# A two-block transformer kernel with a PEER layer on one core: gate tables read earlier, last picks before dots, gelus later among the picks, third tile first at the end

## The chip, the cores and the metric

One core of a Trainium2 chip runs the whole kernel. The metric is the device time of one execution in microseconds (us); lower is better. A run's time is given as the median of several executions; the profile is one more execution, whose span runs from its first instruction to its last.

## The reference, cut to what matters

The input is one sequence of 512 tokens by 1024. Two blocks are computed one after the other, in float32. The first has two kinds of attention and a dense feed-forward layer, the second an mLSTM, a differential attention and a PEER layer; a final norm ends it. All that the change touches is the PEER layer and the norm behind it:

```python
q = (xb @ w_query).reshape(TOKEN_BLOCK, P_HEADS, 2, P_HALF)
s = jnp.einsum('thpk,hpnk->thpn', q, sub_keys).astype(jnp.float32)
sv, si = lax.top_k(s, P_TOPK)
...
fv, fpos = lax.top_k(cand, P_TOPK)
eidx = jnp.take_along_axis(cidx, fpos, axis=-1)
g = jax.nn.softmax(fv, axis=-1)
u = u_tab[eidx]
act = jax.nn.gelu(jnp.einsum('td,thkd->thk', xb, u).astype(jnp.float32), approximate=False)
return jnp.einsum('thk,thkd->td', (g * act).astype(xb.dtype), v_tab[eidx])
```

Each token picks 128 of 16384 experts (8 heads of 16), each expert a row `u` and a row `v` of 1024 numbers. The 512 tokens are four tiles of 128, numbered 0 to 3. The layer's output is multiplied by `g2` and added to `x`, and the sum goes through an rmsnorm.

## The kernel before, in words

The program is written out by hand for five engines and their queues, with semaphores between them; nothing reorders it. The engines are PE (matmuls), ACT (activations), DVE (vector work), POOL (which issues the indirect gathers) and SP (which only issues transfers).

The PEER layer treats its four token tiles in two ways.

**Picks, tiles 0 and 1.** For each of the 256 picks (2 tiles of 128, `NPICK`), POOL gathers one row of `u` and `v` together for each of 128 tokens, 1 MiB in all, into one of 8 slots (`rows`, line 2351). DVE takes the dot product (`dot`, line 2176), ACT the gelu and its product with the gate (`weights`, lines 1815 and 1816), and DVE adds the weighted `v` row to the tile's sum (`value`, line 2194) three picks later. The slot is then free, and POOL gathers the pick that comes 8 later into it. The first 39 picks (`NEARLY`) belong to an earlier stretch of 20 beats (`NBEAT`), and their values are added by PE with diagonal matrices (`values`, line 1552).

**Dense chunks, tiles 2 and 3.** All 16384 experts are computed for these 256 tokens, in 128 chunks (`NCHUNK`) of 128 experts. Per chunk `c` the work is:

- SP loads a turned `u` block (512 KB, `ubuf`, three buffers, lines 1322 and 1342) and a `v` block (512 KB, `vbuf`, three buffers, line 1325).
- PE makes the dots of chunk `c + 16` (`dense_dots`, line 1591; `AHEAD` is 16).
- ACT takes the gelu of a pair of chunks `m`, that is chunks `2m` and `2m + 1` (`dense_gelu`, line 1844). It waits for the dots of the pair and for the values of the chunk 16 before, whose weights lie in the same buffer (`d_done`).
- DVE multiplies the pair with its gates (`dense_weights`, line 2229). The gates come from 64 tables that PE makes in the last 8 beats (`gate_tables`, line 1614). ACT copies them and stores them to DRAM (line 1837), and SP reads them back as 16 blocks of 1 MiB, each with the gates of 8 chunks (`load_gates`, line 1328).
- PE multiplies the weights with the `v` block into banks 2 to 5, tile 2 into banks 2 and 3 (`td` 0) and tile 3 into banks 4 and 5 (line 1644).

The dots of the first 16 chunks are made ahead of chunk 0: ten in the beats, and chunks 10 to 15 in the last beat, behind its last gate table. The last four early picks, 35 to 38, are added by PE behind those six.

**What ties picks to chunks** is the order on ACT and DVE. `pick_at(c)` is 39 + 1.8 c, the pick that is due at chunk `c`:

```python
while m < NCHUNK // 2 and pick_at(2 * m + 1 - AHEAD) <= n:
    dense_gelu(m)
...
while m < NCHUNK // 2 and n >= max(NEARLY + 2 + m, pick_at(2 * m + 1 - 9)):
    dense_weights(m)
```

The first is ACT's loop over the picks `n` and runs ahead of `weights(n)`; the second is DVE's and runs behind `dot(n)`. PE's dots of chunk `2m + 4` wait for the gelu of pair `m`, whose PSUM bank they overwrite.

At chunks 114 and 118 PE turns `x` of tiles 2 and 3, and ACT copies them behind picks 246 and 253 (line 1887). At the end DVE closes each tile in four steps (`last`, lines 2233 to 2258): times `g2`, plus `x`, sum of squares, and behind ACT's square root the product with the gain. SP stores the tile.

Of the kernel before, what the change touches and what calls it, by code (L numbers as in the profile page):

```python
# [49 lines left out]
NGT = 2  # L50
# [3 lines left out]
AHEAD = 16  # L54
# [35 lines left out]

QBEAT = 9
DOT_PAIRS = {11: 1, 12: 1, 13: 1, 14: 1, 15: 1, 19: 3}
DOT_PAIR0, _seen = {}, 0
# [111 lines left out]
def build(nc, ap, out, gates_in_dram):  # L205
    with ExitStack() as ctx:
# [1082 lines left out]
        s_done, s_ev, w_ok, d_done = sem("dense_dots"), sem("dense_gelu"), sem("dense_weights"), sem("dense_values")  # L1289
        a_pool = sem("first_one_hots_pool")  # L1290
        x_copied = sem("x_copied")
        g2_pe, g2_ev = sem("g2_pe"), sem("g2_ev")
# [18 lines left out]
        def _(sp):  # L1311
            sp.wait_ge(ada_first[3], 16)
            for n in range(NBLK):
                if n >= 2:
                    sp.wait_ge(mm_done, MM_THROUGH[n - 2])
                sp.dma_start(ring[n % 2][:, :], ap["wstream"][n]).then_inc(w_loaded[n % 2], 16)
            for j in range(AHEAD + 3):
                if j == 0:
                    sp.wait_ge(mm_done, MM0["pq"] + 1)
                if j >= 3:  # L1320
                    sp.wait_ge(s_done, j - 2)
                sp.dma_start(ubuf[j % 3], ap["u_turned"][j]).then_inc(u_loaded[j % 3], 16)

            def load_values(j):
# [11 lines left out]
            load_gates(1)  # L1336
            load_values(2)
            for c in range(NCHUNK):
                if c + AHEAD + 3 < NCHUNK:
                    sp.wait_ge(s_done, c + AHEAD + 1)  # L1340
                    j = c + AHEAD + 3
                    sp.dma_start(ubuf[j % 3], ap["u_turned"][j]).then_inc(u_loaded[j % 3], 16)
                if c + 3 < NCHUNK:
                    sp.wait_ge(d_done, c + 1)
                    load_values(c + 3)
                if c % 8 == 0 and c // 8 + 2 < 16:
                    sp.wait_ge(w_ok, 4 * (c // 8 + 1))
                    load_gates(c // 8 + 2)
                if c == 100:
                    sp.wait_ge(fin_ok, 1)  # L1350
                    sp.dma_start(out[0:P, :], acc[0]).then_inc(stored, 16)
# [7 lines left out]
        def _(pe):  # L1359
# [196 lines left out]
            for i, (half, c) in enumerate(QUERIES):  # L1556
# [12 lines left out]
                if i % 2 == 0 and i >= 2:  # L1569
                    key_scores(i // 2 - 1)  # L1570
                if i == 6:
                    pe.wait_ge(tt_ev, 1)
                    for b in range(2):
                        ins = turn(hT, 1, b, 6 + b)
                    ins.then_inc(tt_pe, 1)
                if i == 9:
                    pe.wait_ge(tt_ev, 2)
                    for k in range(KD):
                        ins = pe.matmul(PS[:, 6 + k // 4, tile(k % 4)], modc2[:, 40 + k:41 + k].to_broadcast([P, P]), ident,
                                        start=True, stop=True)  # L1580
                    ins.then_inc(g2_pe, 1)
# [41 lines left out]
            for b in range(QBEAT, NBEAT):  # L1623
# [6 lines left out]
                for g in beat_tables(b):  # L1630
                    gate_tables(g)
            beat_dots(NBEAT - 1)
            values(beat_picks(NBEAT - 1))

            pe.wait_ge(picks_ev, 2)
            pe.wait_ge(g_ev, 64)
            for c in range(NCHUNK):
                if c + AHEAD < NCHUNK:
                    dense_dots(c + AHEAD)
                pe.wait_ge(w_ok, c // 2 + 1)  # L1640
                pe.wait_ge(vt_loaded[c % 3], 16 * (c // 3 + 1))
                for td in range(2):
                    for half in range(2):
                        ins = pe.matmul(bank(2 + 2 * td + half), weights_of(c)[:, tile(td)], vbuf[c % 3][:, half * 512:half * 512 + 512],  # L1644
                                        start=(c == 0), stop=(c == NCHUNK - 1))
                ins.then_inc(d_done, 1)
                if c in (4, 80):
# [7 lines left out]
                if c in (114, 118):  # L1655
# [4 lines left out]
                    for half in range(2):  # L1660
                        ins = turn(xT, 2 + c // 118, half, half)
                    ins.then_inc(x_turned, 1)


        @block.scalar
        def _(act):
# [128 lines left out]
            def copy_query(i):  # L1795
# [4 lines left out]
                if i >= 2 and i % 2 == 0:  # L1800
                    copy_scores(i // 2 - 1)
                if i in (1, 6):
                    t = i // 6
                    act.wait_ge(tt_pe, t + 1)
                    act.activation(h2tok[t].rearrange("p (a n) -> p a n", a=2), PS[:, 6:8, :], ACT.Copy).then_inc(tt_ev, 1)
                if i == 9:
                    act.wait_ge(g2_pe, 1)
# [63 lines left out]
            for n in range(NEARLY, NPICK):  # L1871
                while m < NCHUNK // 2 and pick_at(2 * m + 1 - AHEAD) <= n:
                    dense_gelu(m)
                    m += 1
# [19 lines left out]
        def _(dve):  # L1894
# [336 lines left out]
            def last(t, step):  # L2231
                a = halves(acc[t])
                ss = ssf[t]
                if step == 0:
# [3 lines left out]
                    else:  # L2238
                        dve.wait_ge(d_done, NCHUNK)
                        own(dve.tensor_tensor(a, PS[:, 2 * t - 2:2 * t, :], g2row[:, :, :], ALU.mult))  # L2240
# [40 lines left out]
            for n in range(NEARLY, NPICK):  # L2281
                dot(n)
                while done < min(n + 1 - lag_of(n), NPICK):
                    value(done)
                    done += 1
                while m < NCHUNK // 2 and n >= max(NEARLY + 2 + m, pick_at(2 * m + 1 - 9)):
                    dense_weights(m)
                    m += 1
# [8 lines left out]
            while m < NCHUNK // 2:  # L2297
                dense_weights(m)
                m += 1
            for t, step in ((1, 0), (1, 1), (1, 2), (1, 3), (2, 0), (2, 1), (2, 2), (3, 0), (3, 1), (3, 2), (2, 3), (3, 3)):  # L2300
                last(t, step)
# [178 lines left out]
```

## Time and profile before

| What | us |
|---|---|
| Median of 3 runs (all: 2657.36, 2665.32, 2668.45) | 2665.32 |
| The profiled execution, its own time | 2658.6 |
| Its span, first to last instruction | 2655.9 |
| PE busy | 2491.8 (94%) |
| DVE busy | 1485.2 (56%) |
| ACT busy | 602.3 (23%) |
| POOL busy | 432.5 (16%) |
| Moved by the transfers | 592.31 MB, mean 223 GB/s |

Busy shares are over the whole span. The rows in the section below are of the stretch that the change touches, from about 1700 us to the end; in them a matmul in float32 has two records, and so has a dot on DVE, so that a count of 8 on line 1644 is one chunk and a count of 16 on line 1591 one chunk's dots.

### The profile page before, as it was taken

What the parts mean: (1) busy time and instruction counts of PE and PEld (TensorE: products, weight loads), DVE (VectorE), ACT (ScalarE), POOL (GpSimd) and SP (SyncE); (2) the same over time, 40 slices, a digit from 0 to 9 for tenths busy, and PEclk for the clock granted to TensorE, in tenths of its full rate; (3) what the DMA queues carried; (4) which work ended last, traced back from release to release, by engine and by line L of the source; (5) the groups of instructions that cost most, each with busy time, mean ns of one, the idle gap of its engine ahead of it and who ended that gap; (6) DMA issues with size and microseconds to landing.
All of it is one profiled execution on the core that took longest, in us unless ns stands there. A gap on an engine that the chain in (4) does not pass through costs nothing.

```text
span 2655.9 us, 24709 instructions
## 1 busy us (share of the span) xinstructions
PE 2491.8 (94%) x8808; PEld 1431.0 (54%) x8808; DVE 1485.2 (56%) x3368; ACT 602.3 (23%) x1482; POOL 432.5 (16%) x351
## 2 busy tenths in 40 slices
PE   6999999999999999999998887799999999999997
PEld 3454555444444444444467665666665666656563
DVE  5444454220105424223657799847686877777777
ACT  2022364110000002222422245501111112111111
POOL 0000000000000000000000155523333333333331
PEclk9999999999999999999999998999999999999999
DMA  9531011112127521111032376889999999999996
GB/s 378 230 119 60 36 48 48 64 67 91 63 108 302 196 90 64 63 64 64 16 143 104 112 280 238 300 356 415 412 417 406 417 416 417 414 417 415 416 396 259
DMA packets 120740, 592.31 MB, mean 223 GB/s; under 512 B 10000, under 2 KB 42768, under 8 KB 76592
## 3 DMA queue, kind: packets, MB, share of 16 engines
q0 software_dynamic: 40656, 321.93, 29.9%
q1 hardware_dynamic: 46224, 247.48, 24.1%
q10 hardware_dynamic: 33744, 21.40, 2.7%
q8 instruction: 67, 1.10, 0.2%
q14 instruction: 49, 0.40, 0.0%
HBM read 571.90 MB, written 18.87 MB: 222 GB/s over the span
## 4 chain that ended last, share of the span: by engine, by line
PE 79%; DMA 10%; DVE 8%; ACT 1%; issue 1%; POOL 0%; DVEq 0%; ACTq 0%; POOLq 0%
PE PS L622 25%; PE PS L1591 13%; PE PS L1644 13%; PE PS L652 8%; DMA arena<-in_u_turned 5%; PE PS L1164 4%; DMA arena<-in_peer_uv 4%; PE PS L1210 3%; PE PS L807 2%; PE PS L1552 1%; PE PS L827 1%; PE PS L816 1%; DMA arena<-in_ada 1%; DVE arena L2219 1%; PE PS L1185 1%; PE PS L1614 1%
## 5 line engine op out<-in xcount | busy, mean ns | idle before, releaser
L1591 PE MATMUL PS<-hT,arena 128*128 128x256 f32 x2048 | 479.6, 389 | 32.6 <-DMA arena<-in_u_turned 32.5
L1591 PEld LDWEIGHTS PS<-hT,arena 128*128 128x128 f32 x2048 | 397.7, 195 | 146.8 <-DMA arena<-in_u_turned 55.5
L2351 POOL DMA_INDIRECT arena<-in_peer_uv,arena x163 | 219.3, 1346 | 1000.2 <-DVE arena L2147 470.2
L622 PE MATMUL PS<-arena,ring 128*128 128x512 f32 x832 | 359.2, 593 | 2.1 <-issue 0.8
L622 PE MATMUL PS<-hT,ring 128*128 128x256 f32 (+1 forms) x928 | 302.7, 486 | 2.9 <-ACT hT L442 2.9
L622 PEld LDWEIGHTS PS<-arena,ring 128*128 128x128 f32 x832 | 157.0, 190 | 203.2 <-issue 201.9
L622 PEld LDWEIGHTS PS<-hT,ring 128*128 128x128 f32 x928 | 179.6, 195 | 122.4 <-issue 105.0
L2194 DVE SCALAR_TENSOR_TENSOR arena<-arena 128x1024 f32<-128x1024 f32 x134 | 171.8, 1282 | 129.3 <-ACT arena L1816 129.1
L1644 PE MATMUL PS<-arena,hT 128*128 128x512 f32 x512 | 231.5, 595 | 6.3 <-DMA arena<-in_peer_uv 4.6
L1644 PE MATMUL PS<-arena,ring 128*128 128x512 f32 x512 | 230.1, 593 | 1.4 <-DMA arena<-in_peer_uv 0.8
L2176 DVE CUSTOM_DVE_ANT_0 arena<-arena 128x1024 f32<-128x1024 f32 x163 | 198.3, 1221 | 44.9 <-DMA arena<-in_peer_uv,arena 44.3
L652 PE MATMUL PS<-hT,ring 128*128 128x512 f32 x512 | 221.5, 595 | 1.7 <-ACT hT L442 1.7
L652 PEld LDWEIGHTS PS<-hT,ring 128*128 128x128 f32 x512 | 97.8, 191 | 124.9 <-issue 123.6
L2351 POOL DMA_INDIRECT ring<-in_peer_uv,arena x93 | 118.3, 1273 | 246.3 <-DVE arena L2194 195.2
L2318 POOL DMA_DIRECT2D arena<-in_ada x20 | 10.5, 528 | 896.2 <-ACTq L406 665.0
L1644 PEld LDWEIGHTS PS<-arena,hT 128*128 128x128 f32 x512 | 95.3, 190 | 110.5 <-issue 108.5
L1644 PEld LDWEIGHTS PS<-arena,ring 128*128 128x128 f32 x512 | 96.4, 190 | 102.7 <-issue 99.6
L2194 DVE SCALAR_TENSOR_TENSOR arena<-ring,arena 128x1024 f32<-128x1024 f32 x81 | 103.9, 1282 | 67.7 <-ACT arena L1816 67.6
L1995 DVE TENSOR_SCALAR arena<-PS 128x512 f32<-128x512 f32 x32 | 22.1, 692 | 195.4 <-PE PS L652 195.4
L1981 DVE SCALAR_TENSOR_TENSOR xT<-PS,modc,xT 128x512 f32<-128x512 f32 x24 | 18.0, 751 | 179.5 <-PE PS L622 179.5
L2176 DVE CUSTOM_DVE_ANT_0 ring<-ring,arena 128x1024 f32<-128x1024 f32 x93 | 113.2, 1220 | 8.1 <-DMA ring<-in_peer_uv,arena 5.6
L1164 PE MATMUL PS<-hT,ring 128*128 128x512 f32 x256 | 115.4, 593 | 0.0
(349 smaller groups left out, 2765.5 us busy)
## 6 DMA issues: line engine op xcount, KB each, us to landing
ring<-in_wstream SPq DMA_DIRECT2D x45, 2048.0 KB, 7.9
arena<-in_u_turned SPq DMA_DIRECT2D x128, 512.0 KB
arena<-in_peer_uv SPq DMA_DIRECT2D x128, 512.0 KB, 14.7
arena<-in_ada POOLq DMA_DIRECT2D x24, 2048.0 KB, 9.7
gate_tables<-arena ACTq DMA_DIRECT2D x16, 1024.0 KB, 5.3
arena<-gate_tables SPq DMA_DIRECT2D x16, 1024.0 KB, 15.7
arena<-in_peer_uv,arena POOLq DMA_INDIRECT x163
xT<-in_xT POOLq DMA_DIRECT2D x1, 2048.0 KB, 18.9
```

Of the source, the lines that this page charges most:

```text
L622: ins = pe.matmul(o, l, r, start=(a == 0), stop=(a == len(lhs) - 1))
L652: ins = pe.matmul(bank(j % 2, n), w[:, k, m * P:(m + 1) * P], act_in(k), start=(k == 0), stop=(k == kc - 1))
L807: ins = pe.matmul(o, l, r, start=True, stop=True)
L816: ins = pe.transpose(o, l, ident[0:n, 0:n])
L827: ins = pe.matmul(o, l, r, start=start, stop=stop)
L1164: ins = pe.matmul(bank(7), w[:, k, tile(j % 4)], hT[:, k, :], start=(k == 0), stop=(k == KD - 1))
L1210: ins = pe.matmul(bank(5 + j % 2), lhs, rhs, start=(k == 0), stop=(k == KD - 1))
L1591: ins = pe.matmul(dense_bank(j), ubuf[j % 3][:, tile(k)], hT[:, k, 256:512], start=(k == 0), stop=(k == KD - 1))
L1644: ins = pe.matmul(bank(2 + 2 * td + half), weights_of(c)[:, tile(td)], vbuf[c % 3][:, half * 512:half * 512 + 512], start=(c == 0), stop=( ...
L2176: dve.tensor_tensor_reduce(u, u, h2tok[t], 1.0, 0.0, ALU.mult, ALU.add, dots[:, e:e + 1]).then_inc(dot_ok, 1)
L2194: ins = dve.scalar_tensor_tensor(out=a, in0=v, scalar=wexp[:, t, e:e + 1], in1=a, op0=ALU.mult, op1=ALU.add)
L2351: pool.indirect_dma_start(rows[j], None, ap["peer_uv"], bass.IndirectOffsetOnAxis(ap=eidx[:, t, e:e + 1], axis=0)).then_inc(landed[j], 16)
```

## The change

Five edits, all of order; no instruction is added but for one more semaphore.

1. **Turns of tokens.** In the queries' loop PE turns the tokens of tile 1 behind query 3 instead of 6, and `g2` behind query 5 instead of 9. ACT's copies of them move alike.
2. **SP's queue.** The `u` blocks 0 to 12 are issued as before. Then come `v` block 0, gate block 0, `v` block 1, gate block 1 and `v` block 2, and only then the `u` blocks 13 to 18, which wait for the dots of chunks 10 to 15.
3. **Last early picks.** PE adds the values of picks 35 to 38 before the dots of chunks 10 to 15.
4. **Gelus and their products.** ACT's place for `dense_gelu(m)` is `pick_at(2m + 1 - 12)`, was `- 16`; DVE's for `dense_weights(m)` is `pick_at(2m + 1 - 7)`, was `- 9`.
5. **The end.** In the last three chunks (`LAST`) PE does tile 2's half alone; tile 3's three halves follow. DVE waits for tile 2's matmuls with a semaphore of their own, and does all of tile 2's steps before tile 3's.

```diff
-            for j in range(AHEAD + 3):
-                if j == 0:
-                    sp.wait_ge(mm_done, MM0["pq"] + 1)
+            def load_first_rows(j):
                 if j >= 3:
                     sp.wait_ge(s_done, j - 2)
                 sp.dma_start(ubuf[j % 3], ap["u_turned"][j]).then_inc(u_loaded[j % 3], 16)
+
+            sp.wait_ge(mm_done, MM0["pq"] + 1)
+            for j in range(2 * DOT_PAIR0[NBEAT - 1] + 3):
+                load_first_rows(j)
...
             load_gates(1)
             load_values(2)
+            for j in range(2 * DOT_PAIR0[NBEAT - 1] + 3, AHEAD + 3):
+                load_first_rows(j)
...
-                if i == 6:
+                if i == 3:
                     pe.wait_ge(tt_ev, 1)
...
-                if i == 9:
+                if i == 5:
                     pe.wait_ge(tt_ev, 2)
...
+            values(beat_picks(NBEAT - 1))
             beat_dots(NBEAT - 1)
-            values(beat_picks(NBEAT - 1))
...
-                for td in range(2):
-                    for half in range(2):
...
-                ins.then_inc(d_done, 1)
+                ins = second_rows(c, 0)
+                if c == NCHUNK - 1:
+                    ins.then_inc(d_first, 1)
+                if c < NCHUNK - LAST:
+                    second_rows(c, 1).then_inc(d_done, 1)
...
+            for c in range(NCHUNK - LAST, NCHUNK):
+                second_rows(c, 1).then_inc(d_done, 1)
...
-                while m < NCHUNK // 2 and pick_at(2 * m + 1 - AHEAD) <= n:
+                while m < NCHUNK // 2 and pick_at(2 * m + 1 - 12) <= n:
                     dense_gelu(m)
...
-                while m < NCHUNK // 2 and n >= max(NEARLY + 2 + m, pick_at(2 * m + 1 - 9)):
+                while m < NCHUNK // 2 and n >= max(NEARLY + 2 + m, pick_at(2 * m + 1 - 7)):
...
-            for t, step in ((1, 0), (1, 1), (1, 2), (1, 3), (2, 0), (2, 1), (2, 2), (3, 0), (3, 1), (3, 2), (2, 3), (3, 3)):
+            for t, step in ((1, 0), (1, 1), (1, 2), (1, 3), (2, 0), (2, 1), (2, 2), (2, 3), (3, 0), (3, 1), (3, 2), (3, 3)):
```

How the instructions stand on SP around the last gate table. In the names, `in_u_turned` is a `u` block, `in_peer_uv` a `v` block and `gate_tables` a gate block; `dense_dots` is the semaphore of the chunks' dots. Before:

```order
L1322 DMA arena<-in_u_turned 128x1024 [waits dense_dots] x16
L1325 DMA arena<-in_peer_uv 128x1024 [waits gate_tables]
L1328 DMA arena<-gate_tables 128x2048 [waits gate_table_stored1,gate_table_stored0]
L1325 DMA arena<-in_peer_uv 128x1024
L1328 DMA arena<-gate_tables 128x2048
L1325 DMA arena<-in_peer_uv 128x1024
L1342 DMA arena<-in_u_turned 128x1024 [waits dense_dots]
```

And now:

```order
L1322 DMA arena<-in_u_turned 128x1024 [waits dense_dots] x10
L1329 DMA arena<-in_peer_uv 128x1024 [waits gate_tables]
L1332 DMA arena<-gate_tables 128x2048 [waits gate_table_stored1,gate_table_stored0]
L1329 DMA arena<-in_peer_uv 128x1024
L1332 DMA arena<-gate_tables 128x2048
L1329 DMA arena<-in_peer_uv 128x1024
L1322 DMA arena<-in_u_turned 128x1024 [waits dense_dots] x6
L1348 DMA arena<-in_u_turned 128x1024 [waits dense_dots]
```

Six loads of `u` blocks have moved behind the five reads of values and gates.

PE behind the last gate table (line 1614). Line 1591 is the dots of a chunk, line 1552 the value of an early pick. Before, with the six chunks' dots cut to the first and the last:

```order
L1614 MATMUL PS<-arena 128x128 x3
L1591 MATMUL PS<-hT,arena 128x256 [waits dense_gelu,u_loaded1]
...
L1591 MATMUL PS<-hT,arena 128x256 [waits u_loaded0]
L1591 MATMUL PS<-hT,arena 128x256 x7
L1552 MATMUL PS<-ring,arena 128x512 [waits diagonals]
```

And now, where these lines are 1620, 1597 and 1558:

```order
L1620 MATMUL PS<-arena 128x128 x3
L1558 MATMUL PS<-ring,arena 128x512 [waits diagonals]
...
L1558 MATMUL PS<-arena 128x512 [waits diagonals]
L1558 MATMUL PS<-arena 128x512
L1597 MATMUL PS<-hT,arena 128x256 [waits dense_gelu,u_loaded1]
```

The four picks' values stand ahead of the six chunks' dots.

The last two gelus on ACT (pairs 62 and 63), up to the copy of tile 2's `x` (line 1887). Line 1844 is the gelu of a pair, lines 1815 and 1816 are one pick, and the pick that also waits for `gates` is pick 240. Before:

```order
L1844 ACTIVATE ring<-PS 128x512 [waits dense_values,dense_dots]
L1815 ACTIVATE arena<-arena 128x1 [waits dots]
L1816 ACTIVATE arena<-arena 128x1 [waits act_own]
...
L1844 ACTIVATE ring<-PS 128x512 [waits dense_values,dense_dots]
...
L1815 ACTIVATE arena<-arena 128x1 [waits dots,gates]
...
L1887 ACTIVATE arena<-PS 128x1024 [waits x_turned]
```

And now, where these lines are 1858, 1829, 1830 and 1901:

```order
L1829 ACTIVATE arena<-arena 128x1 [waits dots,gates]
...
L1858 ACTIVATE ring<-PS 128x512 [waits dense_values,dense_dots]
...
L1858 ACTIVATE ring<-PS 128x512 [waits dense_values,dense_dots]
L1829 ACTIVATE arena<-arena 128x1 [waits dots]
L1830 ACTIVATE arena<-arena 128x1 [waits act_own]
L1901 ACTIVATE arena<-PS 128x1024 [waits x_turned]
```

Both gelus stood ahead of pick 240 and stand behind it now; between the last gelu and the copy there were nine picks and is one.

## Rows read from the trace of the kernel before

**Rows 1.** The page's 40 slices of the span: PE and transfers, in tenths
```profile
PE   6999999999999999999998887799999999999997
DMA  9531011112127521111032376889999999999996
```
**Rows 2.** Stretches: length, busy of each engine (count), clock, DMA share, GB/s
```profile
1720.00:2579.20 859.20, 823.75 (x2807) 537.17 (x2806) 616.90 (x1111) 149.88 (x507) 281.18 (x203) 0.98 1.01 409
1718.00:1745.00 27.00, 27.00 (x112) 20.94 (x111) 0.46 (x2) 3.06 (x6) 2.89 (x3) 1.00 0.65 213
1748.00:1758.00 10.00, 10.00 (x34) 6.27 (x33) 4.48 (x7) 0.00 (x0) 0.94 (x1) 1.00 1.02 425
```
**Rows 3.** Stretches again, the long middle and the two of the end
```profile
1760.00:2570.00 810.00, 774.55 (x2624) 502.43 (x2623) 607.52 (x1098) 146.98 (x500) 273.60 (x196) 0.98 1.02 415
...
2579.20:2621.40 42.20, 37.31 (x98) 16.29 (x96) 32.60 (x41) 9.94 (x35) 12.74 (x10) 1.00 0.98 392
2621.40:2642.30 20.90, 20.82 (x48) 8.98 (x48) 13.17 (x17) 2.48 (x6) 0.00 (x0) 1.00 0.41 134
```
**Rows 4.** Up to 2579.2, line 2176 alone: DVE busy (dots, two records each)
```profile
0.00:2579.20 2579.20, 295.54 (x484) 0.98 0.57 222
```
**Rows 5.** Up to 2579.2, line 1644 alone: PE and PEld busy (chunks, eight records each)
```profile
0.00:2579.20 2579.20, 404.52 (x897) 168.30 (x898) 0.98 0.57 222
```
**Rows 6.** Up to 1717.6 and up to 2579.2, line 2351 alone: POOL busy (gathers issued)
```profile
0.00:1717.60 1717.60, 43.74 (x43) 0.98 0.35 128
...
0.00:2579.20 2579.20, 324.92 (x246) 0.98 0.57 222
```
**Rows 7.** Who waited for whom, 1745 us to the end: total, times, longest
```profile
ACT hT L1844 <- PE PS L1644: 365.9, 28, 19.8
POOL arena L2351 <- DVE arena L2194: 352.0, 128, 11.7
ACT ring L1844 <- PE PS L1644: 278.3, 24, 16.9
...
DVE arena L2194 <- ACT arena L1816: 196.7, 51, 12.6
...
PE PS L1591 <- DMA arena<-in_u_turned: 32.5, 9, 5.0
```
**Rows 8.** Order of time, 1713 to 1752 us: start, us, engine, line, idle before
```profile
1717.63 20.89 PE L1591 MATMUL PS<-hT,arena 128*128 128x256 f32 x96
...
1718.92 0.37 ACTq L1837 DMA_DIRECT2D gate_tables<-arena  x1
1721.28 17.59 SPq L1322 DMA_DIRECT2D arena<-in_u_turned  x6
...
1738.35 3.60 PE L1552 MATMUL PS<-ring,arena 128*128 128x512 f32 x8
...
1740.50 0.99 POOL L2351 DMA_INDIRECT ring<-in_peer_uv,arena  x1 [23.93 <-PE PS L1552]
...
1747.54 0.69 DVE L2229 TENSOR_TENSOR hT<-hT,arena 128x512 f32<-128x512 f32 x1 [29.08 <-DMA arena<-gate_tables]
```
**Rows 9.** The chain that ended last, in order of time: start, us, what
```profile
2107.58 3.47 PE PS L1591 x16
2111.06 22.48 DMA arena<-in_u_turned
...
2195.46 3.43 PE PS L1644 x8
2198.90 3.45 PE PS L1591 x16
...
2609.16 0.87 PE PS L1530 x8
```
**Rows 10.** Order of time, from 2621 us: start, us, engine, line, idle before
```profile
2621.38 20.84 PE L1644 MATMUL PS<-arena,ring 128*128 128x512 f32 x48 [0.17 <-DMA arena<-in_peer_uv]
...
2629.59 1.22 DVE L2237 TENSOR_TENSOR arena<-arena,sq 128x1024 f32<-128x1024 f32 x1
...
2633.99 1.28 DVE L2257 SCALAR_TENSOR_TENSOR arena<-arena,smalls 128x1024 f32<-128x1024 f32 x1
...
2642.26 1.22 DVE L2240 TENSOR_TENSOR arena<-PS,sq 128x1024 f32<-128x1024 f32 x1 [6.98 <-PE PS L1644]
...
2651.54 1.28 DVE L2257 SCALAR_TENSOR_TENSOR arena<-arena,smalls 128x1024 f32<-128x1024 f32 x1
```

**Rows 11.** ACT in order of time, 1380 to 1400 us, beside the queries
```profile
1384.40 1.02 ACT L1805 ACTIVATE arena<-PS 128x1024 f32<-128x1024 f32 x1 [0.28 <-PE PS L1530]
...
1391.31 0.38 ACT L1799 ACTIVATE arena<-PS 128x256 f32<-128x256 f32 x1 [3.07 <-PE PS L622]
```

More of the change, by code:

```diff
@@ L91 @@
 QBEAT = 9
+LAST = 3
 DOT_PAIRS = {11: 1, 12: 1, 13: 1, 14: 1, 15: 1, 19: 3}
@@ L1290, in build @@
         a_pool = sem("first_one_hots_pool")
+        d_first = sem("dense_values_first_tile")
         x_copied = sem("x_copied")
@@ L1631, in _, with second_rows @@
                     gate_tables(g)
+            values(beat_picks(NBEAT - 1))
             beat_dots(NBEAT - 1)
-            values(beat_picks(NBEAT - 1))
             pe.wait_ge(picks_ev, 2)
             pe.wait_ge(g_ev, 64)
+            def second_rows(c, td):
+                for half in range(2):
+                    ins = pe.matmul(bank(2 + 2 * td + half), weights_of(c)[:, tile(td)], vbuf[c % 3][:, half * 512:half * 512 + 512],
+                                    start=(c == 0), stop=(c == NCHUNK - 1))
+                return ins
             for c in range(NCHUNK):
@@ L1641, in _ @@
                 pe.wait_ge(vt_loaded[c % 3], 16 * (c // 3 + 1))
-                for td in range(2):
-                    for half in range(2):
-                        ins = pe.matmul(bank(2 + 2 * td + half), weights_of(c)[:, tile(td)], vbuf[c % 3][:, half * 512:half * 512 + 512],
-                                        start=(c == 0), stop=(c == NCHUNK - 1))
-                ins.then_inc(d_done, 1)
+                ins = second_rows(c, 0)
[3 more added lines that the diff above has]
+                    second_rows(c, 1).then_inc(d_done, 1)
                 if c in (4, 80):
@@ L1801, in copy_query @@
                     copy_scores(i // 2 - 1)
-                if i in (1, 6):
-                    t = i // 6
+                if i in (1, 3):
+                    t = i // 3
                     act.wait_ge(tt_pe, t + 1)
                     act.activation(h2tok[t].rearrange("p (a n) -> p a n", a=2), PS[:, 6:8, :], ACT.Copy).then_inc(tt_ev, 1)
-                if i == 9:
+                if i == 5:
                     act.wait_ge(g2_pe, 1)
@@ L2238, in last @@
                     else:
-                        dve.wait_ge(d_done, NCHUNK)
+                        if t == NGT:
+                            dve.wait_ge(d_first, 1)
+                        else:
+                            dve.wait_ge(d_done, NCHUNK)
                         own(dve.tensor_tensor(a, PS[:, 2 * t - 2:2 * t, :], g2row[:, :, :], ALU.mult))
```

## The prediction

> **What bounds the kernel now.** I read the slices first. From about 1740 us PE and the transfers both stand at nine tenths or more [rows 1], so either could be the bound. The stretches decide it. Between 1720 and 2579.2 us, the end of chunk 111 (897 records of line 1644 are 112 chunks [rows 5]), 859.2 us at 409 GB/s moved 351 MB [rows 2]. That can be counted out of the program: 115 `v` blocks and 115 `u` blocks of 0.524 MB, 16 gate blocks of 1.049 MB, and gathers 43 to 245, which are 203 of 1.049 MB [rows 6], make 350 MB, and one table's store makes 351. PE's own work is shorter. A chunk is 3.45 us of dots and 3.43 us of values [rows 9], 6.88 us, and PE idled 35 of 810 us [rows 3]. What a chunk must move, 1.05 MB of blocks, 0.13 of gates and 1.8 gathers of 1.05, is 3.07 MB, or 7.4 us at the 415 GB/s of [rows 3]. So up to chunk 111 the kernel is bound by bytes, not by a wait, and a reordering gains there only where the transfers were idle.
>
> Two places are left. From 1718 to 1745 the transfers were busy 0.65 of 27 us [rows 2], so 9.5 us were idle. At the end it turns round. Behind chunk 111 PE has 16 chunks without dots left, 16 x 3.43 = 54.9 us and two turns of 0.87 [rows 9]. The first ten and both turns took 42.2 us [rows 3] where PE's work is 36.0, because the last ten gathers were still coming in; the last six ran as one block of 20.84 us [rows 10] with the transfers at 0.41 [rows 3]. Bytes moved before chunk 111 ends cost their full time; bytes left for later cost little.
>
> The waits look like something else. ACT waited 644 us for PE in front of gelus [rows 7], and so DVE for ACT and POOL for DVE. That says only that the picks always stood as far ahead of the chunks as ACT's order lets them.
>
> **Edit 1, the early turns: 0.** The moved copies are 1.02 us on an ACT that idles about 3 us between two queries' copies [rows 11], and PE's work is the same. First used they are only at query 11.
>
> **Edits 2 and 3, the front: -2.5 us.** Before, the gathers of picks 43 to 46 waited for the four values that PE put behind 20.89 us of dots: POOL idled 23.93 us until 1740.5. SP's reads of gates stood behind `u` block 18, and DVE idled 29.08 us for them [rows 8]. Now PE does the four values from 1717.6 to 1724.5, so four gathers leave 20 us earlier, and SP asks for the gates once the last table, on its way since 1718.9 [rows 8], has landed. But the queue is not free: `u` blocks 13 to 15 now stand behind 3.7 MB. From 1718 until block 15 has landed, 5.2 MB of blocks and gates and 4.2 MB of gathers go through, 22.7 us at 415 GB/s; with the store ahead of them this ends near 1747. Dots 13 start then at about 1744.5 and dots 15 end at 1755, against 1738.5 before. On ACT the gelus of pairs 5 to 7 stand ahead of pick 39's weight, so no value is added and no gather beyond pick 46 leaves before 1756 or so. From 1747 to 1758 only `u` blocks 16 to 18 move, 3.8 us of bytes: some 7 us idle in place of 9.5. Ends: -9.5 if everything is filled, +3 if block 13 lands 5 us later. I take the count. PE starts chunk 0 ten microseconds later, which its 35 us of idle time covers; without them it would cost those 10.
>
> **Edit 4, the later gelus: +17.7 and -6.2.** Gelu `m` waits for chunk `2m - 15`. Before, it stood at the pick due at chunk `2m - 15`, now at the one due at `2m - 11`. The picks may so run four chunks, 7.2 picks, further ahead, and as they stood at this limit all the way [rows 7] I expect them to take it. At the end of chunk 111 gelu 63 held pick 238: 242 dots were done [rows 4] and 246 gathers issued [rows 6]. Now it holds pick 246, value 245 has freed its slot, and 254 are issued. The last four of them leave at the end of chunk 109, two chunks of 6.88 us earlier, time for 5.7 MB of which 2.1 are blocks, so one may still be under way. Seven more gathers ahead of the end of chunk 111 are 7.3 MB or 17.7 us (ends: 0 if the picks don't move ahead, 20.2 for eight). Behind it, three gathers are left and not ten, and the 42.2 us shrink to PE's 36.0: -6.2 (ends -6.2 and 0). PE's dots need a gelu from chunk `2m - 12` on, so ACT must now be over one chunk ahead; at the new limit it has two to spare. DVE's products come two chunks later in the picks, covered by the same lead.
>
> **Edit 5, the end: -4.4 us.** From PE's last matmul both tiles took DVE from 2642.26 to 2652.82 [rows 10], 10.6 us. One tile alone, by tile 1's steps from 2629.59 to 2635.27 [rows 10], takes 5.7. Tile 2's matmuls now end 3 x 3.43 / 2 = 5.1 us before PE's end, so its 5.7 us run 0.5 past it and tile 3's 5.7 follow: 6.2 in place of 10.6. Ends: -5.1 and 0 (DVE still busy with picks, which it was until 2629.6 [rows 10]).
>
> **Sum:** -2.5 + 17.7 - 6.2 - 4.4 = +4.6 us. The profiled execution took 2658.6, so it would take 2663.2. It lies 6.7 below the median of the three runs, which spread over 11; the mean of the four is 2662.4, and from it I give **2667**.
>
> **Rivals.**
>
> *The picks stay where they were* (the lead is not taken): -2.5 - 4.4 = -6.9, or -13.9 with the front wholly filled; from 2662.4 that is 2655.5 and 2648.5. It would need gathers that get less than their 61% of the bytes. Against it: while PE waited for one 0.5 MB block it took 22.48 us [rows 9], so the gathers crowd the blocks out. Chance 0.18.
>
> *The transfers go faster when they come less in bursts.* 425 GB/s stands in one stretch against 415 in the long one [rows 2, 3]; 2.4% of 810 us is -19.4, with the sum -14.8: 2647.6. Against it: the share is 1.01 to 1.02 all the way, with nothing to fill. Chance 0.09. The Trainium skill, DMA: Bandwidth & Descriptors, Specifications, gives 435 GB/s as the ceiling of the fabric. By that the stretch is 5% from full, and an estimate from that figure is 37 us of gain in place of the 19.4; no row here shows 435 held.
>
> *Not what it says* (the lead and the stalls cancel, or only the end's edit works): 0 to -4.4, 2658 to 2662. Chance 0.13.
>
> *Slower: the lead is paid in full and nothing comes back.* Eight gathers, +20.2, crowd out `u` blocks 126 and 127 and the `v` blocks of chunks 112 to 114, PE enters the last 16 chunks with empty buffers and stalls as before (0), and the front, where pick 39 waits for `u` block 15, gives 0: with the end's edit +15.8, so 2678. It decides from the point where lead and front together cost 17.7 more than the stalls give back. For it: before, `v` blocks came in late down to chunk 121. Chance 0.15.
>
> **How the numbers follow.** A measurement of this kernel can tell about 0.5%, 13.3 us, from no change. Forecast 0.45, rivals 0.18, 0.09, 0.13 and 0.15. Faster by over 13.3 us: most of the second rival and part of the first, 0.16. Slower by over that: two thirds of the last rival and the forecast's upper ends, 0.13. The rest, 0.71, is within. The range 2650 to 2681 leaves out most of the second rival and the last one's extreme.
>
> **What would show it.** In the profile after: the wait of 29 us for the gate tables on DVE and POOL's of 24 gone, but a wait of PE for a `u` block at dots 13 and transfers nearly idle around 1750; gelus waiting for PE as before; at the end of chunk 111 about 250 dots and 254 gathers, at about 2594; then all 16 chunks in 57 us; 6.2 us of DVE behind PE's last matmul. The forecast is wrong if the count of gathers there is still about 246, or if the middle moves more than 420 GB/s.

## The result, and the profile after

The changed kernel takes **2679.86 us** (median of 6 runs, 2673.52 to 2681.16), the kernel before 2663.82 (6 runs, 2657.36 to 2668.45). The ratio is 1.0056, 95% interval 1.0046 to 1.0066: slower by 12.3 to 17.6 us. The forecast was 2667, 4.6 us more than its base of 2662.4. The time lies inside the range, but where the slower rival had put it (2678), and with parts that neither had summed.

| What | us |
|---|---|
| The profiled execution, its own time | 2679.83 |
| Its span | 2678.0 |
| PE busy | 2500.6 (93%) |
| DVE busy | 1485.2 (55%) |
| ACT busy | 603.7 (23%) |
| POOL busy | 420.7 (16%) |
| Moved by the transfers | 592.33 MB, mean 221 GB/s |

The profiled execution of before (2658.6) was a short one for its kernel, 5 us under the median of 2663.8. From the last gate table to the end of chunk 111 it took 861.4 us; the two experiments that are before's up to there (the turns alone and the end alone) took 868.4 and 870.4, but their profiled executions lay 2 and 7 us over their own medians. A difference between two profiles in this stretch is thus known to some 9 us only. The rates of the first 80 us and the counts agree far better.

Stretches of after. The first is the 80 us behind the last gate table, the next two are inside it, then come the picks' first long stretch, the middle, all of it up to the end of chunk 111, and the 42.2 us behind that, as in [rows 2, 3].

```profile
1721.30:1801.30 80.00, 68.86 (x255) 49.38 (x255) 36.31 (x62) 10.96 (x37) 16.54 (x15) 0.91 0.85 324
...
1745.00:1755.00 10.00, 5.36 (x13) 4.30 (x14) 0.19 (x2) 0.00 (x0) 0.00 (x0) 0.50 0.63 259
...
1765.00:1780.00 15.00, 15.00 (x55) 10.19 (x54) 14.77 (x21) 2.92 (x13) 6.14 (x5) 1.00 0.87 326
...
1840.00:2100.00 260.00, 239.54 (x794) 152.85 (x793) 197.72 (x359) 47.25 (x159) 82.90 (x65) 0.97 1.02 416
...
1760.00:2570.00 810.00, 772.25 (x2609) 499.58 (x2608) 615.23 (x1107) 150.44 (x503) 266.65 (x199) 0.98 1.01 411
...
1721.00:2610.30 889.30, 835.29 (x2820) 542.84 (x2819) 638.30 (x1138) 157.30 (x525) 282.82 (x211) 0.97 1.00 405
...
2610.30:2652.50 42.20, 42.20 (x111) 19.52 (x111) 25.67 (x31) 8.33 (x25) 3.35 (x2) 1.00 0.69 226
```

Before, the first and the fourth of these:

```profile
1717.80:1797.80 80.00, 75.05 (x280) 53.13 (x279) 30.29 (x47) 9.29 (x31) 16.23 (x14) 0.98 0.89 348
...
1840.00:2100.00 260.00, 249.86 (x847) 163.54 (x846) 196.32 (x358) 45.58 (x155) 90.32 (x65) 0.97 1.01 413
```

The last column is what to read. The first 80 us moved 324 GB/s in place of 348, which is 1.9 MB or 4.6 us at 415. Between 1840 and 2100 the transfers are as full as before, and PE idles 20 of 260 us in place of 10. It does 33 chunks (794 records, 24 to a chunk with its dots) in place of 35, while POOL and DVE have as many instructions as before: here the picks take part of their lead. Behind chunk 111 PE never idled in 42.2 us, where it idled 4.9 before [rows 3].

What was done at the end of chunk 111, at 2610.3: dots on DVE (two records each), chunks on PE (eight each), gathers on POOL, as in [rows 4 to 6].

```profile
0.00:2610.30 2610.30, 305.20 (x500) 0.98 0.57 222
...
0.00:2610.30 2610.30, 404.97 (x897) 168.14 (x898) 0.98 0.57 222
...
0.00:2610.30 2610.30, 325.56 (x254) 0.98 0.57 222
```

So 250 dots and 254 gathers, the two counts that the prediction gave. The waits from 1745 us on, as in [rows 7]:

```profile
POOL arena L2368 <- DVE arena L2208: 356.4, 128, 12.8
ACT ring L1858 <- PE PS L1645: 330.5, 28, 20.1
ACT hT L1858 <- PE PS L1645: 253.2, 23, 17.7
...
PE PS L1597 <- DMA arena<-in_u_turned: 50.2, 11, 11.1
POOL arena L2368 <- DVE arena L2202: 36.3, 1, 36.3
```

ACT still waits 584 us for PE before gelus, 644 before; a POOL wait of 36.3 us is new, and so is one of 11.1 us of PE. Both are in the front. Order of time there, as in [rows 8]:

```profile
1721.11 3.60 PE L1558 MATMUL PS<-ring,arena 128*128 128x512 f32 x8
...
1722.40 0.37 ACTq L1851 DMA_DIRECT2D gate_tables<-arena  x1
1723.27 0.99 POOL L2368 DMA_INDIRECT ring<-in_peer_uv,arena  x1 [4.84 <-PE PS L1558]
...
1738.20 0.33 SPq L1332 DMA_DIRECT2D arena<-gate_tables  x1
...
1743.35 0.69 DVE L2243 TENSOR_TENSOR hT<-hT,arena 128x512 f32<-128x512 f32 x1 [21.22 <-DMA arena<-gate_tables]
...
1749.64 16.84 PE L1597 MATMUL PS<-hT,arena 128*128 128x256 f32 x64 [11.14 <-DMA arena<-in_u_turned]
...
1764.11 1.28 DVE L2202 SCALAR_TENSOR_TENSOR arena<-arena,PS 128x1024 f32<-128x1024 f32 x1 [18.93 <-ACT arena L1830]
...
1765.67 0.94 POOL L2368 DMA_INDIRECT arena<-in_peer_uv,arena  x1 [36.31 <-DVE arena L2202]
```

The chain through it:

```profile
1722.40 15.72 DMA gate_tables<-arena
...
1740.34 9.26 DMA arena<-in_u_turned
```

The last table's store took 15.72 us to land. SP stood behind it, then put two `v` and two gate blocks ahead of `u` block 13, and PE waited for that block until 1749.64. Pick 39's value, and with it the next gather, came at 1764 to 1765.7. Before, they came at 1749.3 and 1750.8:

```profile
1749.30 1.28 DVE L2188 SCALAR_TENSOR_TENSOR arena<-arena,PS 128x1024 f32<-128x1024 f32 x1
...
1750.84 0.94 POOL L2351 DMA_INDIRECT arena<-in_peer_uv,arena  x1 [4.25 <-DVE arena L2188]
```

The end, as in [rows 9, 10]: PE's last blocks, the first step of tile 2, and the last step of tile 3.

```profile
2639.33 20.76 PE L1645 MATMUL PS<-arena,ring 128*128 128x512 f32 x48
2661.70 7.10 PE L1645 MATMUL PS<-arena,ring 128*128 128x512 f32 x16 [1.60 <-DMA arena<-in_peer_uv]
```

```profile
2663.69 1.23 DVE L2257 TENSOR_TENSOR arena<-PS,sq 128x1024 f32<-128x1024 f32 x1 [16.84 <-PE PS L1645]
...
2673.70 1.29 DVE L2274 SCALAR_TENSOR_TENSOR arena<-arena,smalls 128x1024 f32<-128x1024 f32 x1
```

DVE runs 6.2 us past PE's last matmul (2668.8 to 2675.0), as forecast. But PE now waits 1.60 us for the last `v` block.

### The profile page after: what moved, and what is told of

Its sections match the earlier page's. It is cut to its first block, busy times and chain, and to the rows that moved or that the text cites. A ratio compares the mean times of both kernels' runs of the same rounds, so it can differ in the third digit from the quotient of the medians.

```text
span 2678.0 us, 24709 instructions
## 1 busy us (share of the span) xinstructions
PE 2500.6 (93%) x8808; PEld 1434.8 (54%) x8808; DVE 1485.2 (55%) x3368; ACT 603.7 (23%) x1482; POOL 420.7 (16%) x351
## 2 busy tenths in 40 slices
DMA packets 120741, 592.33 MB, mean 221 GB/s; under 512 B 10000, under 2 KB 42768, under 8 KB 76592
## 4 chain that ended last, share of the span: by engine, by line
PE 74%; DMA 15%; DVE 8%; ACT 1%; issue 1%; POOL 0%; SPq 0%; DVEq 0%; ACTq 0%; POOLq 0%
PE PS L623 25%; PE PS L1645 11%; PE PS L1597 11%; PE PS L653 8%; DMA arena<-in_u_turned 8%; DMA arena<-in_peer_uv 5%; PE PS L1165 4%; PE PS L1211 3%; PE PS L808 2%; PE PS L828 1%; PE PS L817 1%; DMA arena<-in_ada 1%; DVE arena L2233 1%; PE PS L1558 1%; PE PS L1186 1%; PE PS L1620 1%
```

## The experiments

Theory: the parts have the prices of the prediction, and the front is worth little either way. Rival: the front costs, because what moves ahead holds up what now stands behind. Kernels are timed against before on the same chip. From here on "front" is GB/s in the 80 us behind the last gate table; kernels with the old front have 344 to 348, and I take 347. A front of X costs 80 x (347 - X) / 415 us. The rule is coarse: with the window 4 us later, one kernel's front reads 280 in place of 270, which is 2 us.

### Each part alone

**Edit 4 alone.**

```diff
-                while m < NCHUNK // 2 and pick_at(2 * m + 1 - AHEAD) <= n:
+                while m < NCHUNK // 2 and pick_at(2 * m + 1 - 12) <= n:
...
-                while m < NCHUNK // 2 and n >= max(NEARLY + 2 + m, pick_at(2 * m + 1 - 9)):
+                while m < NCHUNK // 2 and n >= max(NEARLY + 2 + m, pick_at(2 * m + 1 - 7)):
```

> The kernel before with the later gelus and products alone (edit 4). Theory of bytes: the picks run four chunks further ahead, about 254 gathers are issued when chunk 111 ends in place of 246, that end comes 17 to 20 us later, the 16 last chunks take 57 us in place of 63, and the time is 11 to 14 us longer (ratio 1.004 to 1.005). Rival, that the front alone made the change slower: no difference, within 3 us.

Measured: 2675.69 against 2664.45, ratio 1.0045 (1.0032 to 1.0058), +12.0 us. Its stretch behind chunk 111, then dots and gathers up to there:

```profile
2605.40:2662.10 56.70, 56.66 (x144) 25.60 (x143) 25.67 (x31) 8.33 (x25) 3.35 (x2) 1.00 0.58 199
...
0.00:2605.40 2605.40, 305.30 (x500) 0.98 0.57 223
...
0.00:2605.40 2605.40, 325.60 (x254) 0.98 0.57 223
```

The 16 chunks took 56.7 us with PE busy throughout, and the counts are those predicted. The theory of this part holds, with its size.

**Edits 2 and 3 together**, then each alone. Edit 3 is the first hunk, edit 2 the rest.

```diff
-            beat_dots(NBEAT - 1)
             values(beat_picks(NBEAT - 1))
+            beat_dots(NBEAT - 1)
...
-            for j in range(AHEAD + 3):
...
+            for j in range(2 * DOT_PAIR0[NBEAT - 1] + 3):
+                load_first_rows(j)
...
             load_values(2)
+            for j in range(2 * DOT_PAIR0[NBEAT - 1] + 3, AHEAD + 3):
+                load_first_rows(j)
```

> The kernel before with the gate reads ahead of u blocks 13 to 18 and the last picks' values ahead of the dots (edits 2 and 3). Theory: in the profile after, the last gate table's store landed 15.7 us after its issue, beside the gathers that now start 20 us earlier, and the gate reads, u block 13 and pick 39's weight stand behind it; the front idles as much as it gains, so 0 to +4 us, with the transfers idle around 1750 as in the profile after. Rival, that filling the gap pays as meant: -6 to -10 us.

> The kernel before with the last picks' values ahead of the dots alone (edit 3). Theory: four gathers leave 20 us earlier into transfers that were half idle, and u blocks 13 to 18 keep their place, so PE's dots 10 to 15 end at about 1745 without a wait for a block; pick 39's weight moves from 1739 to 1745 only. The 9.5 us of idle time shrink by about 6: -4 to -8 us. Rival, that the gathers hold up the store of the last gate table here too and that this delays chunk 0: 0 or more.

> The kernel before with the gate reads ahead of u blocks 13 to 18 alone (edit 2). Theory, as the front runs so far have it (lone edit 3 idled the transfers 7.8 us more in the first 80 us, edits 2 and 3 together 11.5 us more): without the early gathers the last gate table's store lands in about 6 us, the gate reads start near 1725, u block 13 comes behind them near 1735, so dots 15 end near 1745, and the gathers of picks 43 to 46, behind those dots as before, leave near 1748 and so still cover the wait of gelu 8 for chunk 1. Idle about as before, 0 to +5 us. Rival, that the edit that hurts is this one, not edit 3: +8 us or more.

| Kernel | ratio (95%) | us | front, GB/s | its cost by the rule above |
|---|---|---|---|---|
| edits 2, 3 | 1.0048 (1.0036 to 1.0061) | +12.8 | 281 | 12.7 |
| edit 3 | 1.0035 (1.0023 to 1.0048) | +9.3 | 302 | 8.7 |
| edit 2 | 1.0051 (1.0036 to 1.0067) | +13.6 | 287 | 11.6 |

The theory fails for all three. For edits 2 and 3 together its rival, a gain, failed too; for each edit alone the rival, a cost, had the sign right. Each part alone costs, and both together cost about what either does: the three intervals overlap. Edit 3 alone, 80 us and 15 us of stretches, then order of time (the last row is pick 39's value):

```profile
1720.90:1800.90 80.00, 67.58 (x238) 46.78 (x238) 28.00 (x39) 7.52 (x25) 15.61 (x13) 0.91 0.79 302
...
1765.00:1780.00 15.00, 15.00 (x55) 10.20 (x54) 7.94 (x11) 2.14 (x9) 3.42 (x3) 1.00 0.41 143
```

```profile
1750.64 0.36 SPq L1328 DMA_DIRECT2D arena<-gate_tables  x1
...
1758.70 2.07 PE L1644 MATMUL PS<-arena,hT 128*128 128x512 f32 x2 [5.55 <-DVE hT L2229]
...
1759.70 1.28 DVE L2188 SCALAR_TENSOR_TENSOR arena<-arena,PS 128x1024 f32<-128x1024 f32 x1
```

The dots of chunks 10 to 15 come 7 us later, and so do the `u` loads that wait for them and the gate reads behind those on SP, at 1750.6. Chunk 0 begins at 1758.7. SP did not stand behind the store here, so it is the order on PE and not the store that costs. Then there is a second hole that the prediction did not have: with the old place of gelus, gelu 8 stands early among the picks and waits for chunk 1, and from 1765 to 1780 the transfers are busy 0.41. POOL idled 11.9 us there, until 1774.1. Edit 2 alone, order of time:

```profile
1723.99 0.37 ACTq L1841 DMA_DIRECT2D gate_tables<-arena  x1
1731.05 0.33 SPq L1330 DMA_DIRECT2D arena<-gate_tables  x1
...
1742.49 12.65 PE L1595 MATMUL PS<-hT,arena 128*128 128x256 f32 x48 [9.28 <-DMA arena<-in_u_turned]
...
1757.13 0.99 POOL L2355 DMA_INDIRECT ring<-in_peer_uv,arena  x1 [37.13 <-PE PS L1556]
```

Here the gates are read at 1731, only 7 us behind their store, and yet PE waits 9.28 us for `u` block 13, since SP issued it behind two `v` blocks and two gate blocks. That wait stands in the path of everything: dots, early values, gathers (POOL idle 37 us), chunk 0 at 1765.3.

**Edit 5 alone, and edit 1 alone.**

```diff
+            for c in range(NCHUNK - LAST, NCHUNK):
+                second_rows(c, 1).then_inc(d_done, 1)
```

> The kernel before with the end's edit alone (edit 5): tile 2's matmuls first in the last three chunks. Theory: DVE behind PE's last matmul shrinks from 10.6 to 6.2 us, nothing else moves: -4.4 us (ratio 0.9983). Rival, that DVE is still busy with picks or the split of the last chunks costs PE: 0.

Measured: 2661.39, ratio 0.9991 (0.9981 to 1.0001), -2.4 us where -4.4 was expected. The interval, -5.1 to +0.3 us, shuts out neither 0 nor -4.4; what tells is the profile. From PE's last matmul to the span's end it is 9.3 us, was 13.7. Part of it was given back in front of it:

```profile
2650.13 7.10 PE L1641 MATMUL PS<-arena,ring 128*128 128x512 f32 x16 [1.69 <-DMA arena<-in_peer_uv]
```

The last three chunks' tile 2 halves take 1.7 us each, so PE reaches the last `v` block 3.4 us after it freed that block's buffer; the load takes longer. A wait at the last `v` block is there in the changed kernel (1.60) and with all but edit 4 (1.44) too, and not in before [rows 10]. -4.4 + 1.7 is -2.7.

```diff
-                if i == 6:
+                if i == 3:
```

> The kernel before with the earlier turns alone (edit 1). Theory: the copies lie in ACT's idle time, nothing waits: 0, within 2 us. Rival, that it is behind the 3 to 4 us by which the last gate table ended later in the profile after: +3 to +4 us (but that also stood in the profiles of the runs without edit 1).

Measured: 2664.46, ratio 1.0005 (0.9995 to 1.0016): nothing, as expected.

**All but edit 4.** The changed kernel with both lines of edit 4 put back.

```diff
-                while m < NCHUNK // 2 and pick_at(2 * m + 1 - 12) <= n:
+                while m < NCHUNK // 2 and pick_at(2 * m + 1 - AHEAD) <= n:
```

> The change without edit 4 (edits 1, 2, 3 and 5). Theory: the front's +12 of the run with edits 2 and 3, less the end's 2 to 4: +8 to +10 us, with 246 gathers when chunk 111 ends and about 20 us idle in the first 80. Compared with the whole change (+15) edit 4 then costs only 5 to 7 us here, since it pays back part of the front's second hole, where alone it cost 11. Rival, that the edits add up: +12 - 3 + 0 = +9 as well, but then the whole change would have had to be +20.

Measured: 2673.53 against 2662.62, ratio 1.0040 (1.0025 to 1.0055), +10.7 us. By the ratios edit 4 thus costs some 4 us on top of the others (1.0056 against 1.0040, give or take 5), and 12 alone. The front is 270, a cost of 14.8, where the changed kernel has 324 and 4.4. The reason is the second hole: in this kernel the transfers were busy 0.38 from 1765 to 1780, in the changed one 0.87. Its last table came 5 us earlier, but from 1760 to 1775 the share is 0.43 too. Later gelus let the picks through.

```profile
1765.00:1780.00 15.00, 15.00 (x56) 10.19 (x55) 6.95 (x9) 2.14 (x9) 2.92 (x2) 1.00 0.38 138
```

### Can the parts be put to better use

**Late gelus only at first.** Edits 2 and 3, and edit 4's places up to pair 12, then back by one chunk a pair to the places of before, for gelus and products.

```diff
-                while m < NCHUNK // 2 and pick_at(2 * m + 1 - AHEAD) <= n:
+                while m < NCHUNK // 2 and pick_at(2 * m + 1 - 12 - min(4, max(0, m - 12))) <= n:
```

> Edits 2 and 3 as in the front run, with edit 4's later places for the first pairs only; from pair 12 on they go back to the places of before. Theory: the second hole of the front, where pick weights wait for gelu 8 and this for chunk 1 while all gathers have landed, closes as it did in the change, and the end of chunk 111 has 246 gathers as before: the idle time of the first 80 us falls from 21 to about 13 us and the time from +12 to +3 to +5 us. Rival, that the front costs its 12 us in another way (PE's late chunk 0): +12 stays.

Measured: 2671.21, ratio 1.0032 (1.0019 to 1.0044), +8.5 us, twice what was expected. The front is 321, a cost of 5.0: the later gelus close the second hole here as well. Some of the rest may lie between 1840 and 2100:

```profile
1840.00:2100.00 260.00, 249.85 (x846) 162.42 (x845) 186.11 (x345) 45.63 (x152) 80.31 (x59) 0.98 1.01 408
```

408 against before's 413 is 1.3 MB or 3.1 us. Kernels with nothing changed here go from 410 to 415, so this is at the edge of what can be told. From 1880 to 1900, where the picks fall back, it is 345.

**Gelus earlier than before**, the opposite of edit 4, with edit 5: the offset grows from 16 chunks to 20.

```diff
+                while m < NCHUNK // 2 and pick_at(2 * m + 1 - AHEAD - min(4, (m - AHEAD // 2) // 4)) <= n:
...
+                while m < NCHUNK // 2 and n >= max(NEARLY + 2 + m, pick_at(2 * m + 1 - 13)):
```

> The opposite of edit 4, with edit 5: gelus at the pick due at chunk 2m - 19 (reached stepwise over the first 16 pairs), products at the one due at 2m - 12. Theory of bytes: the picks stay four chunks further back, about 239 gathers are issued when chunk 111 ends in place of 246, that end comes 17 us earlier, the last 16 chunks stall more (gathers still come) and take 68 to 73 us in place of 63, and with the end's edit the time is 8 to 14 us shorter than before (ratio 0.995 to 0.997). Rival, that edit 4's cost was the picks' order as such or the missing overlap of ACT and PE: slower, as any move from the tuned place.

Measured: 2659.60, ratio 0.9991 (0.9980 to 1.0003), where -8 to -14 us were expected. Chunk 111 ended at 2567.4, 849.0 us behind the last table where kernels with the old lead took 861.4 to 870.4: a gain was there. Behind it the span went on for 90.3 us, where those took 74.5 to 76.7, and most of that is one wait:

```profile
2608.45 1.97 PE L1532 MATMUL PS<-cst,xT 128*128 128x128 f32 x8 [12.02 <-ACT arena L1897]
```

At the second turn of `x`, PE waited 12 us for ACT's first copy, which stands behind a pick that now comes late.

**Two chunks earlier, with that copy moved.**

```diff
+                while m < NCHUNK // 2 and pick_at(2 * m + 1 - AHEAD - min(2, (m - AHEAD // 2) // 4)) <= n:
...
-                if c in (114, 118):
+                if c in (114, 124):
...
-                if n in (pick_at(114) + 2, pick_at(118) + 2):
-                    td = int(n > pick_at(114) + 2)
+                if n in (240, 255):
+                    td = int(n > 240)
```

DVE's products stand at `pick_at(2m + 1 - 11)` here.

> As the run with earlier gelus, but two chunks back in place of four, with edit 5, and with tile 3's turn of x moved from chunk 118 to 124 and ACT's copies of x behind picks 240 and 255. In the run before, PE waited 12 us at that turn for ACT's copy behind pick 246. Theory: 243 gathers when chunk 111 ends, 7 to 8 us earlier, no wait at the turn, last 16 chunks 63 to 66 us: -7 to -11 us. Rival, that the last picks' DVE work now sets the end: -3 to -4 only, the end's edit alone.

Measured: 2660.44 against 2662.62, ratio 0.9984 (0.9972 to 0.9996): by the ratio 4.3 us faster than before, by the medians 2.2. It is the one kernel here whose whole interval (-7.5 to -1.1 us) lies below before, one of twelve tried, and edit 5, which it holds, measured -2.4 alone. The wait at the turn is gone. The gain is less than expected since the limit moved to DVE, as the rival had it:

```profile
2636.58 4.06 DVE L2204 SCALAR_TENSOR_TENSOR arena<-arena 128x1024 f32<-128x1024 f32 x3
...
2656.28 1.28 DVE L2270 SCALAR_TENSOR_TENSOR arena<-arena,smalls 128x1024 f32<-128x1024 f32 x1
```

The last values of picks end at 2640.6, and three tiles of closing steps follow without a gap, 17 us of them; PE had ended at 2643.3. Chunk 111 ended 856.0 us behind the last table, and 83.2 us followed it: what the picks gave back before chunk 111, they took behind it.

**A front that does not stall, and the same with the lead brought back.** Edit 3, but the gelus of pairs 5 to 7 stand ahead of picks 42, 44 and 46, and the first four products come five picks later; later gelus at first as above. The second kernel falls back by six chunks in place of four (products by four in place of two), with edit 5 and the moved copies.

```diff
-            m = AHEAD // 2
+            m = DOT_PAIR0[NBEAT - 1]
...
+                while m < NCHUNK // 2 and (42 + 2 * (m - 5) if m < 8 else pick_at(2 * m + 1 - 12 - min(4, max(0, m - 12)))) <= n:
...
+                while m < NCHUNK // 2 and n >= max(NEARLY + (7 if m < 4 else 2) + m, pick_at(2 * m + 1 - 7 - min(2, max(0, m - 12)))):
```

> The front mended: edit 3, with the weights of picks 39 to 41 ahead of gelu 5 and two picks ahead of each of gelus 6 and 7, the products of pairs 0 to 3 five picks later, and later gelus up to pair 12 as in the run that goes back to the places of before. SP's order is that of before. Theory: values 39 to 43 free slots while PE makes dots 10 to 15, so gathers 47 to 51 fill the hole that a lone edit 3 left, and the idle time of the first 80 us falls from 17.5 to 3 to 6 us, below the 9.7 of before: -3 to -7 us. Rival, that chunk 0, later still behind slower gate reads and u blocks, sets the time: +5 or more.

> Both of the last two: the mended front, gelus two chunks back from pair 18 on, the end's edit and the later turn. Theory: the gains add, -10 to -16 us, faster than both kernels. Rival: DVE behind the last pick sets the end, no better than the better of the two.

Measured: 2663.78 against 2662.62, ratio 1.0000 (0.9986 to 1.0014), and 2669.18, ratio 1.0021 (1.0010 to 1.0032). Both missed, the second with its sign. The first one's stretches, then the second's:

```profile
1721.10:1801.10 80.00, 69.32 (x254) 47.64 (x253) 48.37 (x88) 12.04 (x41) 20.39 (x18) 0.94 0.98 387
...
1840.00:2100.00 260.00, 254.64 (x882) 167.90 (x881) 183.91 (x342) 45.38 (x152) 81.32 (x59) 0.99 0.99 401
```

```profile
1840.00:2100.00 260.00, 252.21 (x869) 165.17 (x868) 169.27 (x321) 44.12 (x146) 71.88 (x53) 0.99 0.96 383
```

The front was mended: 387 GB/s for 347 is 7.7 us gained. But 401 for 413 over 260 us is 3.1 MB, 7.5 us, lost. In 20 us steps the loss is one hole, right where the picks fall back by four chunks within four pairs: 250 GB/s from 1860 to 1880, 385 from 1880 to 1900, and 413 to 418 after it. PE was busy all 40 us, so it could not do more chunks in that time, and with the picks held back the transfers were left without work. In the second kernel the hole is longer (248, 341, 321 and 345 GB/s from 1860 to 1940). With earlier gelus than before, where four chunks were handed back over 16 pairs, there was no such hole: 412 GB/s with PE busy 259.8 of the same 260 us. The fronts of these kernels differ too, so that the pace alone makes the hole is likely and not shown.

For the second kernel the rule of bytes does not close. 30 GB/s over 260 us would be 18.8 us lost, against some 8 for the front and 7.6 for three picks fewer (243 gathers) at chunk 111. But chunk 111 ended 861.9 us behind the last table, as in before (861.4) and 6 to 9 us sooner than in the two other kernels with the old lead. Behind it 84.1 us followed in place of 74.5 to 76.7. There the rival came true: DVE's last value ends at 2646.8, 17 us of closing steps follow without a gap, and PE ends at 2649.3.

## Where the prediction was right and where it was wrong, point by point

**What bounds the kernel: right.** Up to chunk 111 it is bytes: 405 GB/s over 889.3 us are 360 MB, against 351 before, and 8 dots more, whose rows have landed, are 8.4 MB. In the four kernels with edits 2, 3 or both and the old gelus, the bytes of the first 80 us, turned into time at 415 GB/s, give the measured difference within 2 us (for the one with edit 5 too, 14.8 less 2.7 against 10.7). Chunk 111 ended at 2610.3 and not at about 2594: 3.5 us of it are a later last table, which over all fourteen profiles ends between 1716.0 and 1722.9 whatever the edits, the rest the front and the short base.

**Edit 1, 0: right** (1.0005, with its interval).

**Edits 2 and 3, -2.5: wrong, and the step that failed.** The prediction put it so: "with the store ahead of them this ends near 1747. Dots 13 start then at about 1744.5 and dots 15 end at 1755", and "some 7 us idle in place of 9.5". The trace has dots 13 at 1749.64 and pick 39's value, which waits for dots 15 and ACT, at 1764.11. By its front of 324 the changed kernel lost 4.4 us here in place of gaining 2.5. Two things were missing.

- The store was not ahead of the gathers. It shared with them, took 15.72 us, and SP stood behind it. The prediction's own bound allowed block 13 to be 5 us late, and it was; but that bound ended at +3, when the pick's value and so the next gather came 8 us and more after the 1756 that it had. From 1753 to 1757 nothing moved at all.
- The idle time was counted only up to about chunk 0 (1758). With gelus in their old place there is a second hole behind it, at gelu 8. It is why the front costs 12.8 us without edit 4; with it, 4.4 by the front's rate. The signs had it in part: PE's wait at dots 13 and the idle transfers around 1750 came. But DVE's wait for the gates, which was to be gone, fell only from 29.08 to 21.22, and in place of POOL's 23.93 stands one of 36.31.

**Edit 4, +11.5: right.** Alone +12.0 (8.5 to 15.5), with 250 dots and 254 gathers, and 56.7 us for 16 chunks where 57 were given. In the changed kernel they took 58.5, the difference being edit 5's wait. That the picks take any lead they are given held in both directions: 254 gathers at chunk 111 with later gelus, 246 before, 239 with earlier ones. The stretch from the last table to chunk 111 was 884.9 us with edit 4 alone, 861.4 to 870.4 before, and 849.0 with earlier gelus. That is +15 to +24 and -12 to -21 us, which fits 2.5 us for each 1 MiB pick and does not measure it better.

**Edit 5, -4.4: half right.** DVE's part came out as worked out; PE's wait for the last `v` block, which it had at nothing, took 1.6 of it. Measured -2.4.

**The sum.** Put together from what the runs show, front 4.4, gelus 12.0 and end -2.9 are +13.5; measured were +12.3 to +17.6. The forecast's +4.6 was short by 7 us of front, 1.5 of end and 0.5 of gelus; that leaves 1.5 us, within the interval.

**The rivals.** "The picks stay where they were" fell by the counts. "The transfers go faster" fell: the middle went at 411 GB/s, before at 415 [rows 3]. The Trainium skill, DMA: Bandwidth & Descriptors, Specifications, gives 435 GB/s as the fabric's ceiling; in no kernel of this study does a stretch of 200 us go above 417. None of the orders tried here won any of the 4% that are left to it. The slower rival gave the right time from the wrong parts: the stalls behind chunk 111 did come back in full, and the front, which it had at 0, cost in their place. The range held because it reached to that rival; that the time fell into it was luck.

## What to carry to other kernels

Where a queue is bound by bytes, judge a reordering by the bytes moved in the stretch it touches, over a window long enough to hold the second hole, and not by the wait that it removes. When a load is moved ahead of another on a queue that blocks on waits, ask for the last event that the new front load needs (here a store's landing beside gathers), since everything behind it, and the engine that feeds on that, inherits it. Where one stream has a lead over another and the transfers are full, hand it back slowly, no faster than the other stream's engine can use the bytes: here four chunks within four pairs left a hole, four over 16 pairs did not. And look at where the lead comes due: each pick left for later is DVE's work at the end.

## What was not expected of the hardware

- **A store beside gathers.** The same 1 MiB store of the last table took 15.72 us to land with four gathers issued behind it (14.43, 16.11 and 15.98 in three other kernels with edit 3). With edit 2 alone, where no gather is issued for 33 us behind it, SP got past it after 7.06 us (1723.99 to 1731.05), and the median of the 16 is 5.3. So it is the gathers that hold it up. Why it gets so small a share is argued only, from the queues in the page of the changed kernel's profile (the gathers' first, then the one that carries the stores):

```profile
q0 software_dynamic: 40656, 321.93, 29.7%
...
q10 hardware_dynamic: 33744, 21.40, 2.7%
```

  That is 7.9 KB a packet against 634 bytes, each the mean of its whole queue.
- **The clock behind a wait.** PE waited 11.14 us for `u` block 13. The granted clock stood at half, 1.2 in place of 2.4 GHz, from 1742 until 1753, and was full from 1757:

```profile
1742.00:1746.00 4.00, 0.00 (x0) 0.00 (x0) 1.83 (x3) 0.00 (x0) 0.00 (x0) 0.50 1.01 422
...
1749.60:1753.00 3.40, 3.36 (x8) 2.74 (x9) 0.00 (x0) 0.00 (x0) 0.00 (x0) 0.50 0.49 196
1753.00:1757.00 4.00, 4.00 (x14) 3.32 (x14) 0.00 (x0) 0.60 (x1) 0.00 (x0) 0.72 0.00 0
1757.00:1761.00 4.00, 4.00 (x20) 3.51 (x20) 0.00 (x0) 0.00 (x0) 0.00 (x0) 1.00 0.54 157
```

The four chunks' dots took 16.84 us, where four sixths of the 20.89 in [rows 8] are 13.9: for PE the wait cost 11.1 us and 2.9 more.

**What stays open.** A front with the gates read early but `u` block 13 ahead of the other reads was not tried, nor a store in larger packets, nor a slow handing back of the picks' lead behind the mended front. That the last 1.5 us of the sum have no place is within what the runs can tell.
